# A PEER layer on one core: the experts' output rows as dense panels instead of gathers, and part of the key dots on TensorE

## What is computed

```
u = peer_u[eb]                                   # (tokens, 128, 2048)
a = gelu(einsum('td,tkd->tk', xb, u))            # a dot with each expert's input row
return einsum('tk,tkd->td', wb * a, peer_v[eb])  # the weighted sum of their output rows
```

## Time and profile before

| what | value |
|---|---|
| three runs | 2492.22, 2495.73, 2496.10 us |
| median | 2495.73 us |
| span of the profiled execution (its own time is not given apart) | 2493.0 us |
| TensorE busy | 2130.5 us (85%) |
| VectorE busy | 1364.1 us (55%) |
| ScalarE busy | 688.4 us (28%) |
| GpSimd busy | 650.3 us (26%) |
| moved by DMA | 747.14 MB, mean 300 GB/s |

### The profile page before, as it was taken

The page is one execution under the profiler, slowest core; times in us unless marked ns, Lnnn a source line. Parts: engine busy times, 40 slices in busy tenths (PEclk is TensorE's granted clock), DMA queues, the critical chain, the costliest instruction groups (busy, mean ns, idle before and its releaser), DMA issues.

```text
span 2493.0 us, 27387 instructions
## 1 busy us (share of the span) xinstructions
PE 2130.5 (85%) x9752; PEld 1439.3 (58%) x9754; DVE 1364.1 (55%) x1917; ACT 688.4 (28%) x1013; POOL 650.3 (26%) x558
## 2 busy tenths in 40 slices
PE   7999999999999999999977777777777777777776
PEld 5888999998889888888832222222223222222222
DVE  5444455554445555556866565555645555565445
ACT  4444444334444444455301111111111101111001
POOL 0000000000000000001466543545354544554432
PEclk9999999999999999999989999999999999999999
DMA  5454465556565555546999999999999999999996
GB/s 159 134 144 143 135 194 178 185 182 189 185 196 182 186 187 191 174 151 259 366 419 421 422 421 422 421 422 421 421 422 421 421 422 421 422 421 421 421 422 265
DMA packets 214701, 747.14 MB, mean 300 GB/s; under 512 B 16704, under 2 KB 65984, under 8 KB 148416
## 3 DMA queue, kind: packets, MB, share of 16 engines
q0 software_dynamic: 73872, 537.95, 52.0%
q1 hardware_dynamic: 140736, 207.96, 26.4%
HBM read 743.77 MB, written 2.10 MB: 299 GB/s over the span
## 4 chain that ended last, share of the span: by engine, by line
PE 48%; DMA 43%; issue 4%; DVE 2%; POOL 1%; ACT 1%; POOLq 0%; DVEq 0%; ACTq 0%; SPq 0%
PE ps L355 47%; DMA v_rows<-in_peer_v,idx_all 40%; DMA u_rows<-in_peer_u,idx_all 2%; POOL v_rows L1597 1%; DMA raw<-in_peer_wq 1%; ACT hi L769 1%; DVE junk L1439 0%; POOL u_rows L1588 0%; DVE lo L1097 0%; PE ps L440 0%; DVE st L1131 0%; ACT tok L769 0%; PE ps L510 0%; PE ps L488 0%; DVE hm L1214 0%
## 5 line engine op out<-in xcount | busy, mean ns | idle before, releaser
L355 PE MATMUL ps<-v_rows,diag 128*128 128x512 f32 x1984 | 927.1, 612 | 316.4 <-DMA v_rows<-in_peer_v,idx_all 275.3
L355 PEld LDWEIGHTS ps<-v_rows,diag 128*128 128x128 f32 x1984 | 363.1, 192 | 879.0 <-DMA v_rows<-in_peer_v,idx_all 483.5
L1439 DVE SCALAR_TENSOR_TENSOR junk<-u_rows,h 128x2048 bf16<-128x2048 f32 x256 | 583.8, 2292 | 486.4 <-DMA u_rows<-in_peer_u,idx_all 486.3
L1097 DVE TENSOR_TENSOR lo<-raw,hi 128x1024 fp32r<-128x1024 f32 x368 | 448.7, 1225 | 492.5 <-ACT hi L769 491.5
L769 ACT ACTIVATE hi<-raw 128x1024 fp32r<-128x1024 f32 x376 | 397.3, 1059 | 571.0 <-PE ps L355 559.7
L355 PE MATMUL ps<-xh,hi 128*128 128x256 f32 (+2 forms) x1536 | 440.6, 287 | 2.5 <-ACT qkv L769 1.3
L355 PE MATMUL ps<-xh,lo 128*128 128x256 f32 (+2 forms) x1536 | 435.7, 284 | 0.0
L355 PE MATMUL ps<-xl,hi 128*128 128x256 f32 (+2 forms) x1536 | 435.0, 283 | 0.0
L1597 POOL DMA_INDIRECT v_rows<-in_peer_v,idx_all x256 | 310.8, 1214 | 439.9 <-PE ps L355 383.7
L1588 POOL DMA_INDIRECT u_rows<-in_peer_u,idx_all x256 | 317.3, 1239 | 272.7 <-PE ps L355 83.2
L769 ACT ACTIVATE diag<-ident,coef 128x128 f32<-128x128 f32 x256 | 97.7, 399 | 860.2 <-PE ps L355 796.8
(11 more groups left out here) (206 smaller groups left out, 1649.8 us busy)
## 6 DMA issues: line engine op xcount, KB each, us to landing
raw<-in_w_in SPq DMA_DIRECT2D x96, 1024.0 KB, 5.4
raw<-in_w_in SPq DMA_DIRECT2D x64, 256.0 KB, 3.2
raw<-in_w_in SPq DMA_DIRECT2D x32, 512.0 KB, 4.7
raw<-in_p_a SPq DMA_DIRECT2D x16, 1024.0 KB, 5.0
raw<-in_p_b SPq DMA_DIRECT2D x16, 1024.0 KB, 5.1
raw<-in_w_o SPq DMA_DIRECT2D x16, 1024.0 KB, 5.1
raw<-in_peer_wq SPq DMA_DIRECT2D x16, 1024.0 KB, 5.9
u_rows<-in_peer_u,idx_all POOLq DMA_INDIRECT x256, 36.3
```

The costliest lines, as they stand in the source:

```text
L355: return nc.tensor.matmul(o, a, b, start=start, stop=stop)
L1097: V.tensor_tensor(raw_lo[:, hh // 2, k4, :] if kept else lo[:, hh % SLOT_N, :, :], raw[:, hh // 2, k4, :], (kept_hi(hh) if kept else hi[:, ...
L1439: V.scalar_tensor_tensor(junk[:, k % 2, :], u_rows[k % (RING if u else HEAD_RING)][:, :], 1.0, h1[:, u // PH, :], ALU.mult, ALU.mult, accu ...
```

## The change

v is given as two arrays. `peer_v` holds its first 1344 columns (`FD`), `v_gathered` the other 704 (`GD`).

- **Dense part.** All 16384 experts' rows are read in order, as 128 panels of 128 experts by 1344 columns (0.69 MB each, by SyncE). Each panel is split into high and low float32r parts and multiplied on TensorE with a matrix W that holds, for each expert and each token, the coefficient or zero: 18 products a panel (two tiles, three products, column cuts of 512, 512 and 320). The sums of both tiles stay in six PSUM banks.
- **W.** Expert e is 128 i + j. For each token VectorE writes two one-hot matrices over its 128 slots, one of i times the coefficient and one of j (`one_hots`), and TensorE multiplies them (`place`); ScalarE copies four tokens' results at a time into W (`w_copy`). The tokens of tile 0 are placed 16 a unit during units 8 to 15, after each pair below; those of tile 1 after the last unit. W is split high and low two panels at a time.
- **Gathered part.** 256 gathers of 704 columns (0.36 MB) into a ring of 4 (`VRING`), scaled and added to the tokens on VectorE (`add_row`), all in the panel stage.
- **Dots.** From unit 2 on, slots 0, 1, 5, 6, 10 and 11 of a unit go to TensorE in pairs (`dots_pair`): per pair 32 transposes of a 128 by 128 block, eight copies of 512 columns on ScalarE, 16 float32 products of 256 columns against the turned tokens. VectorE takes the diagonal of the result (`pair_dots`). The other ten stay on VectorE, in the order `DVE_ORDER`.
- The diagonal matrices, the products with gathered v rows, the gathers of v beside those of u, and the norm of tile 0 beside tile 1 are gone. Both tiles' last norm comes at the end, and `y2` holds both.

```
 RING = 8
 HEAD_RING = 4
-DRING = 4
+PAIRS = ((0, 1), (5, 6), (10, 11))
+PE_SLOTS = tuple(k for pair in PAIRS for k in pair)
+PE_FROM = 2
+DVE_ORDER = (2, 3, 4, 0, 1, 7, 8, 9, 12, 13, 5, 6, 14, 15, 10, 11)
+BLOCKS = KT // 2
+FD = 1344
+GD = D - FD
+CUTS = ((0, 512), (512, 1024), (1024, FD))
+RAWS, HIS, WBUFS = 4, 3, 2
+VRING = 4
+OHR = 5
+WTOK = (6, 5, 5)
+WB = 4
...
+            for i in range(NKEY):
+                j = i % RAWS
+                if i == 0:
+                    sp.wait_ge(S("dots_done"), PH * TOPK)
+                    sp.wait_ge(S("tile_opened"), 1)
+                    sp.wait_ge(S("h1t_turned"), 4)
+                elif i < RAWS:
+                    sp.wait_ge(S("topk_done"), NT * PH)
+                else:
+                    sp.wait_ge(S("panel_done"), i - RAWS + 1)
+                set_apart(sp)
+                sp.dma_start(v_raw[j][:, :], peer_v[i * P:(i + 1) * P, :]).then_inc(vr_in[j], 16)
+                if i == NKEY - 8:
...
+            def dots_pair(u, pair):
+                T, m = u // PH, pair_number(u, pair)
+                o = ps[:, 5 - 3 * (m % 2), 0:256]
+                def turn(b):
+                    g = m * BLOCKS + b
+                    if g >= 2:
+                        pe.wait_ge(S("ut_copied"), g - 1)
+                    for n in range(2):
+                        for r, k in enumerate(PAIRS[pair]):
+                            kt = 2 * b + n
+                            last = nc.tensor.transpose(ps[:, 3 + g % 2, (2 * n + r) * P:(2 * n + r + 1) * P],
+                                                       u_rows[k % RING][:, kt * P:(kt + 1) * P], ident[:, :])
+                    last.then_inc(S("ut_turned"), 1)
+                def products(b):
+                    g = m * BLOCKS + b
+                    pe.wait_ge(S("ut_copied"), g + 1)
+                    if b == 0 and m >= 2:
+                        before = divmod(m - 2, len(PAIRS))
+                        pe.wait_ge(S("dots_done"), dot_place(before[0] + PE_FROM, PAIRS[before[1]][1]))
+                    for n in range(2):
+                        kt = 2 * b + n
+                        last = mm(o, h1t[T][:, kt, :], ut[:, g % 2, n * 256:(n + 1) * 256], kt == 0, kt == KT - 1)
+                    last.then_inc(S("ut_used"), 1)
+                for k in PAIRS[pair]:
+                    wait_row(pe, u, k)
+                turn(0)
+                for b in range(BLOCKS):
+                    if b + 1 < BLOCKS:
+                        turn(b + 1)
+                    products(b)
+            def slots_turn(T):
+                pe.wait_ge(S("coef_ready"), PH * (T + 1))
...
+            def place(n):
+                b = n // WB
+                bank = 6 + (b + 1) % 2
+                pe.wait_ge(S("oh_ready"), n + 1)
+                if n % WB == 0:
+                    if n % P == WB:
+                        pe.wait_ge(S("slots_copied"), n // P + 1)
+                    if b >= 2:
+                        pe.wait_ge(S("w_evac"), b - 1)
+                mm(ps[:, bank, (n % WB) * P:(n % WB + 1) * P], oh[:, n % OHR, 1, :], oh[:, n % OHR, 0, :], True, True
+                   ).then_inc(S("w_done"), 1)
...
+                    slots_turn(0)
+                for pair in range(len(PAIRS)):
+                    dots_pair(u, pair)
+                    if u >= PH:
+                        for n in w_tokens(u, pair):
+                            place(n)
+            pe.wait_ge(S("dots_done"), 2 * PH * TOPK)
+            pe.wait_ge(S("h1t_copied"), 8)
+            for T in range(NT):
+                tile_open(T)
+            slots_turn(1)
+            for n in range(P, 2 * P):
+                place(n)
...
+            def panel(i):
+                pe.wait_ge(S("vhi_ready"), i + 1)
+                pe.wait_ge(S("vlo_ready"), i + 1)
+                if i % 2 == 0:
+                    pe.wait_ge(S("whi_ready"), NT * (i // 2 + 1))
+                    pe.wait_ge(S("wlo_ready"), NT * (i // 2 + 1))
+                w = w_hl[i // 2 % WBUFS]
+                for T in range(NT):
+                    for wn, v in ((0, v_hi[i % HIS]), (0, v_lo[i % RAWS]), (1, v_hi[i % HIS])):
+                        for n, (a, b) in enumerate(CUTS):
+                            last = mm(ps[:, 3 * T + n, 0:b - a], w[:, wn, T, i % 2, :], v[:, a:b], False,
+                                      i == NKEY - 1 and wn == 1)
+                last.then_inc(S("panel_done"), 1)
+            for i in range(NKEY):
+                panel(i)
...
+            def pair_copies(u, pair):
+                for b in range(BLOCKS):
+                    g = pair_number(u, pair) * BLOCKS + b
+                    act.wait_ge(S("ut_turned"), g + 1)
+                    if g >= 2:
+                        act.wait_ge(S("ut_used"), g - 1)
+                    A(ut[:, g % 2, :], ps[:, 3 + g % 2, :], ACT.Copy).then_inc(S("ut_copied"), 1)
...
+            def w_copy(b):
+                act.wait_ge(S("w_done"), WB * (b + 1))
+                t0 = b * WB % P
+                src = ps[:, 6 + (b + 1) % 2, :].rearrange("p (q i) -> p i q", q=WB)
+                if b * WB < P:
+                    A(wt0[:, :, t0:t0 + WB], src, ACT.Copy).then_inc(S("w_evac"), 1)
+                else:
+                    for j, (i0, i1) in enumerate(W1_PARTS):
...
+            def v_hi_of(i):
+                act.wait_ge(vr_in[i % RAWS], 16 * (i // RAWS + 1))
+                if i >= HIS:
+                    act.wait_ge(S("panel_done"), i - HIS + 1)
+                A(v_hi[i % HIS][:, :], v_raw[i % RAWS][:, :], ACT.Copy).then_inc(S("vhi_ready"), 1)
...
+            for u in range(2, 2 * PH):
+                gelu(u - 2) if u == 2 else None
+                gelu(u - 1)
+                if u == 2:
+                    softmax_exp(1)
+                    softmax_exp(2)
+                if u == PH:
+                    slots_copy(0)
+                for pair in range(len(PAIRS)):
+                    pair_copies(u, pair)
+                    if u >= PH:
+                        while WB * (done + 1) <= w_tokens(u, pair)[-1] + 1:
+                            w_copy(done)
+                            done += 1
+                    if pair == 0 and u + 1 < 2 * PH:
+                        softmax_exp(u + 1)
+            gelu(2 * PH - 1)
+            slots_copy(1)
+            v_hi_of(0)
+            for b in range(done, 2 * P // WB):
+                w_copy(b)
+                if b == 40:
+                    v_hi_of(1)
+                if b == 50:
+                    v_hi_of(2)
...
+            def pair_dots(u, pair):
+                m = pair_number(u, pair)
+                dve.wait_ge(S("ut_used"), (m + 1) * BLOCKS)
+                for r, k in enumerate(PAIRS[pair]):
+                    bank = 5 - 3 * (m % 2)
+                    dve.wait_ge(S("dots_done"), dot_place(u, k) - 1)
+                    V.scalar_tensor_tensor(junk2[:, :], ps[:, bank, r * P:(r + 1) * P], 1.0, ident[:, :], ALU.mult, ALU.mult,
+                                           accum_out=dots[:, u % 2, k:k + 1]).then_inc(S("dots_done"), 1)
...
+            def one_hots(n):
+                t = n % P
+                if n >= OHR:
+                    dve.wait_ge(S("w_done"), n - OHR + 1)
+                V.tensor_scalar(oh[:, n % OHR, 1, :], iota[:, :], slots_t[:, 2, t:t + 1], None, ALU.is_equal)
+                V.tensor_scalar(oh[:, n % OHR, 0, :], iota[:, :], slots_t[:, 1, t:t + 1], slots_t[:, 0, t:t + 1],
+                                ALU.is_equal, ALU.mult).then_inc(S("oh_ready"), 1)
...
+            def v_lo_of(i):
+                dve.wait_ge(S("vhi_ready"), i + 1)
+                V.tensor_tensor(v_lo[i % RAWS][:, :], v_raw[i % RAWS][:, :], v_hi[i % HIS][:, :].bitcast(F32), ALU.subtract
+                                ).then_inc(S("vlo_ready"), 1)
...
+            def add_row(n):
+                T, s = divmod(n, SLOTS)
+                dve.wait_ge(v_in[n % VRING], 16 * (n // VRING + 1))
+                if s:
+                    dve.wait_ge(S("v_added"), n)
+                else:
+                    dve.wait_ge(S("acc_scaled"), T + 1)
+                V.scalar_tensor_tensor(h1[:, T, FD:D], v_rows[n % VRING][:, :], coef_all[:, T, s:s + 1], h1[:, T, FD:D],
+                                       ALU.mult, ALU.add).then_inc(S("v_added"), 1)
             dve.wait_ge(S("const_ready"), 1)
             dve.wait_ge(S("sc_copied"), 1)
...
+                else:
+                    for k in DVE_ORDER:
+                        if not on_pe(u, k):
+                            dot(u, k)
+                        elif k in [p[0] for p in PAIRS]:
+                            pair = [p[0] for p in PAIRS].index(k)
+                            if u >= PH:
+                                if u == PH and pair == 0:
+                                    scale_acc(0)
+                                    wait_slots(0)
+                                for n in w_tokens(u, pair):
+                                    one_hots(n)
```

(118 more changed lines are left out.)

295 lines of the change are left out of this document (124 added, 171 removed).

## The result

The changed kernel takes 2678.34 us (median of 4 runs, 2674.06 to 2685.68) against 2495.55: a ratio of 1.074, with 95% interval 1.072 to 1.076. It is slower, as forecast, but by 183 us where I had 55: the time lies outside the range of 2465 to 2615. The profiled execution spans 2680.1 us.

A forecast was written before the change was run, and what follows sets the result against it. DMA bytes were taken to bound PEER. Unit 7's end at 1523, plus 447 (units 8 to 15), 65.4 (W), 493 (panels) and 20 (tail), gave 2548.5 us; with 2.7 for the median, 2551, range 2465 to 2615.

The forecast's parts named there:

- The chain of units 8 to 15: Token placing between pairs ties top-k, dots, pairs and row 13's gather into one sequence: 56.7 us a unit, 447 in all.
- Units 1 to 7: Units with u gathers and no token placing stay DMA-bound; unit 7's last pair ends at 1523 us.
- a unit now brings 16 MB, 39.8 us: In units 1 to 7, gathers of u alone run at 421 GB/s and set each unit's time, 39.8 us.
- my 11.5 us for a top-k: VectorE's top-k in each unit, counted at 11.5 us within the 36 us of VectorE work of units 1 to 7.
- W of tile 1: Building W for tile 1 after the last unit: 65.4 us, of which 128 tokens at 0.40 make 51.2.
- The panels: The stage of 128 dense panels with gathered v rows: 3.85 us each, 493 us in all.
- four buffers last 7.3 us: Panel stage: after addition and issue, the gather ring leaves 4.0 us for a transfer, so 3.85 us a panel.
- The floor of three full resources, 3.65: Panel stage: TensorE 3.63, VectorE 3.65 and DMA 3.66 us a panel, so at best 3.65.
- the gather ring sets the panel stage: Rival for the panels: every gather late, 4.6 us a panel or more, 2645 us; chance 0.12.
- GpSimd gets through at each end of an operation: Argument against the gather-ring rival: GpSimd can issue when a VectorE operation ends, eight times in two panels.
- Faster: Rival: the token chain costs little, DMA sets units 8 to 15 at 39.8 us; 2422 or 2397 us, chance 0.18.

The follow-up runs named there:

- w_last: Changed kernel with no token of tile 0 placed before unit 15 is done, its W built in one piece afterwards: 2638.43 us, ratio 1.056.
- early_one_hots: Changed kernel with VectorE making the one-hots one group earlier, eight tokens of tile 0 left for after unit 15: 2595.37 us, ratio 1.040.
- two_pairs: As w_last, with 4 of 16 dots of a unit on TensorE instead of 6: 2657.19 us, ratio 1.065.
- all_on_vector: As w_last, with all 16 dots of a unit on VectorE and none on TensorE: 2678.76 us, ratio 1.073.
- u_half_rows: As w_last, with gathers of u fetching 1024 of 2048 columns, which dots and transposes read twice: 2560.75 us, ratio 1.025.

## Why the prediction was wrong

**The chain of units 8 to 15: right in its steps.** Forecast 56.7 us and 447 in all, measured 57.1 and 448. The chain of one unit (start us, us, what held the end):

```profile
1641.62 6.75 DMA u_rows<-in_peer_u,idx_all
1648.39 2.30 DVE junk L1625 x2
1650.69 0.06 DVE ohs L1654
1650.81 0.35 DVE ohs L1655
1651.20 2.60 PE ps L430 x10
1653.81 1.70 PE ps L817 x8
...
1665.28 0.31 DVE junk L1636 x2
...
1665.92 0.22 DVE sc L1573
```

A gather of 6.75 (I had 6.5), the dot of row 13, tokens and their last place, the pair from 1653.81 to 1665.28 with its slow first transposes, diagonals, top-k. That the sum agrees to 0.4 us is partly luck: 0.8 us stands before the gather that I had not counted, and the last pair took 11.5 us where I had 12.7. w_last and early_one_hots confirm the chain from two sides: without the tokens between the pairs, or with their one-hots early, the unit falls to 43.4 and 45.1 us.

**Units 1 to 7: 29 us short.** The failed step is "a unit now brings 16 MB, 39.8 us", with 421 GB/s taken from a stage where u and v were gathered together. There a gather of u needed 36.3 us to land (31.4 to 37.3 between 1700 and 2000 us); the DMA engines had a deep queue. With u alone and eight buffers it lands in 9.9, the share is 0.97 and the rate 385. By share that is 397 GB/s for full engines against 417 before, and 400 to 406 in two_pairs and all_on_vector, where TensorE does less or nothing; so at most 9 of the 20 GB/s go with TensorE's work. u_half_rows, with the share of 0.97, shows the transfers to be the bound. That fewer of them in flight is the reason for the lower rate is argued, not tried. The other part is 4.3 us in the second top-k: `coefs(0)` stands there for a GELU that ScalarE holds back behind its copies, a wait on another engine's order that my 11.5 us for a top-k left out.

**W of tile 1: 10 us short.** The cadence of a token was 0.45, not 0.40:

```profile
2039.85 0.33 DVE L1655 TENSOR_SCALAR ohs<-iota,slots_t 128x128 f32<-128x128 f32 x1
2040.11 0.27 DVE L1654 TENSOR_SCALAR ohs<-iota,slots_t 128x128 f32<-128x128 f32 x1
2040.30 0.33 DVE L1655 TENSOR_SCALAR ohs<-iota,slots_t 128x128 f32<-128x128 f32 x1
```

The operation with two scalar operands takes 0.26 from start to start, the one with one 0.19; I gave both the price of the latter. That is 6 of the 10 us; the rest is not worked out.

**The panels: 91 us short.** The failed step is "four buffers last 7.3 us ... 4.0 us remain for a transfer ... I take 3.85, nearer the floor". The chain of one turn (the mean turn was 9.1 us):

```profile
2302.01 0.96 DVE h L1681
...
2303.02 0.76 issue
2303.78 6.90 DMA v_rows<-in_v_gathered,idx_all
...
2310.70 0.95 DVE h L1681
```

From one addition to that of the fourth row behind it are 8.69 us: 0.96 of addition, 0.8 in which GpSimd stands, 6.90 from issue to landing. I had counted what was left for a transfer and never put a duration beside it, though I used 6.4 us for a transfer by GpSimd in the chain of units 8 to 15. With that same row the turn would have been 0.96 + 0.8 + 6.4, 8.2 us or 4.1 a panel before any jitter. That row is for 1 MB, and a gather of 0.36 MB with nothing beside it took 4.7 us, so it would have come near the 6.5 under load only by luck; but even 4.7 is more than the 4.0 that I had left. The floor of three full resources, 3.65, was not reached by any run that had them all: TensorE alone takes 3.72 (I had 3.63), and the best with everything in it was 4.06. Four buffers left VectorE 114 us idle.

So the rival *the gather ring sets the panel stage*, 4.6 us a panel and a chance of 0.12, was what happened. Its price of 2645 us and the misses of 29 and 10 make 2684, the profiled 2680. "GpSimd gets through at each end of an operation", my argument against it, is true of the trace (the gather issued at 2303.78, inside the low part from 2302.88 to 2304.43, ended at 2305.26 although an addition had followed at once; the gathers of 2200 to 2500 us lasted 1.36 us in the mean, where I had 1.5) and was beside the point, since issue to landing is four fifths of the turn.

**Against the kernel before.** Faster was ruled out for a reason that the forecast had only in part. Bytes fell by 17%, but 75 us without transfers, a stage at 289 GB/s and one at 313 gave back more than they saved. With both repaired, the panels still come at 4.07 to 4.17 us where the bytes alone, at 421 GB/s, needed 3.35.

## What to carry to other kernels

A ring's pace is its turn (issue, landing, use, release) over its buffers; write down the landing time for each ring, with the number from the nearest transfer on the page, before calling any engine the bound, and try one buffer more first. Where an engine waits between long pieces of work for something small made by another, make it one piece earlier: the tokens of tile 0 cost about 100 us in one order and under 25 in the other. A rate read in a stage with a deep queue (421 GB/s) did not hold in one with a quarter of the transfers in flight (385), so take the rate from a stage like the one to be forecast.

## What the hardware showed

- The rate of transfers depends on more than their row size: 217 GB/s at a share of 0.75 for 2816-byte rows alone, 187 at 0.56 for 5376-byte panel loads alone, 354 at 0.96 for both with five buffers. By share the mixture moves 369, more than either by itself (289 and 334).
- A gather of 0.36 MB took 4.7 us to land with nothing beside it and 6.5 to 6.8 with the panel loads.
- A gather's instruction on GpSimd took 0.94 us by itself. With nothing but gathers and additions, 146 of 173 took longer (up to 1.67 us); each of these began during a VectorE addition and ended 0.8 us behind its end.
- TensorE's granted clock was 0.50 (1.2 GHz) from 1250 to 1890 us of all_on_vector, where it had nothing to do. In two_pairs the eight transposes that open a pair took 1.94 us behind a pause of 14 us; in w_last they took 1.06 right behind another pair.
